# A hybrid-attention transformer layer on one core: paced first loads, key sets turned on VectorE

## The reference

```
u = rms_norm(h, g)
q, k_c, v_c, k_s, v_s, k_w, v_w, gate = split(u @ w_in)   # 16 query heads, 4 key/value groups of 128
k_c, v_c = compress(k_c), compress(v_c)                   # blocks of 32 tokens -> 15 compressed rows
k_s = rms_norm(k_s, g1);  k_w = rms_norm(k_w, g2)         # keys of the selected and the window branch
o = gate0*attn(q,k_c,v_c) + gate1*attn(q,k_s,v_s) + gate2*attn(q,k_w,v_w)
h = h + o @ w_out
h = h + square(relu(rms_norm(h) @ mlp_w1)) @ mlp_w2       # 2048 -> 8192 -> 2048
h = h + sigmoid(rms_norm(h) @ w_gate) * (p @ w_proj)
```

## Time and profile before

| | |
|---|---|
| median of 3 runs | 1208.8 us (1207.68 to 1210.01) |
| the profiled execution | 1206.92 us |
| its span, first to last instruction | 1204.8 us |
| TensorE busy | 1194.7 us (99%) |
| VectorE, ScalarE busy | 729.9 us (61%), 591.7 us (49%) |
| DMA in the first 30 us of the page's slices, then | 348 GB/s, then 283 and 210 |

### The profile page before, as it was taken

How to read it: one execution, slowest core, us unless ns; L and a number is a source line. 1 busy time by engine, 2 the same in 40 slices (tenths; PEclk the granted TensorE clock), 3 DMA queues, 4 the chain that set the end, 5 groups by cost and what they waited for, 6 DMA issues and landing times.

```text
span 1204.8 us, 15261 instructions
## 1 busy us (share of the span) xinstructions
PE 1194.7 (99%) x5504; PEld 992.3 (82%) x5504; DVE 729.9 (61%) x956; ACT 591.7 (49%) x812; POOL 70.6 (6%) x63
## 2 busy tenths in 40 slices
PE   8999999999999999999999999999999999999998
PEld 7888788888888888888888888888888888888886
DVE  5676646778766656554465554555555557476554
ACT  7655444666656554443444433445433444455443
POOL 1000000000000011100011100011000012000000
PEclk9999999999999999999999999999999999999999
DMA  9766564333348666765567765677755676785661
GB/s 348 283 210 217 176 202 135 118 106 106 112 152 267 221 222 217 248 226 195 193 211 260 237 207 192 190 242 236 241 192 196 207 242 221 248 263 194 217 206 49
DMA packets 107278, 247.02 MB, mean 205 GB/s; under 512 B 9424, under 2 KB 52432, under 8 KB 107216
## 3 DMA queue, kind: packets, MB, share of 16 engines
q1 hardware_dynamic: 107072, 246.24, 62.5%
q10 hardware_dynamic: 144, 0.01, 0.0%
HBM read 232.58 MB, written 13.63 MB: 204 GB/s over the span
## 4 chain that ended last, share of the span: by engine, by line
PE 94%; DVE 2%; ACT 1%; DMA 1%; SPq 1%; issue 0%; ACTq 0%
PE acc L1425 87%; PE sc L1566 1%; DMA x_raw<-in_x_cols_dram 1%; DVE w_split L947 1%; PE tr L1483 1%; ACT s L698 1%; PE sc L1531 0%; PE tr L1472 0%; PE sc L1472 0%; PE tr L1617 0%; PE tr L1618 0%; SPq L365 0%; PE acc L1455 0%; PE tr L1595 0%; ACT q_split L683 0%
## 5 line engine op out<-in xcount | busy, mean ns | idle before, releaser
L947 DVE TENSOR_TENSOR w_split<-w_raw,w_split 128x1024 fp32r<-128x1024 f32 x411 | 509.7, 1250 | 382.6 <-ACT w_split L597 382.1
L597 ACT ACTIVATE w_split<-w_raw 128x1024 fp32r<-128x1024 f32 x411 | 432.0, 1058 | 419.9 <-PE acc L1425 415.3
L1425 PE MATMUL acc<-w_split,a_hi 128*128 128x512 f32 x1916 | 594.5, 391 | 3.1 <-DVE w_split L947 3.1
L1425 PE MATMUL acc<-w_split,b_split 128*128 128x512 f32 x1920 | 441.0, 390 | 0.0
L1425 PEld LDWEIGHTS acc<-w_split,a_hi 128*128 128x128 f32 x1916 | 356.4, 188 | 78.3 <-issue 4.1
L1425 PEld LDWEIGHTS acc<-w_split,b_split 128*128 128x128 f32 x1920 | 359.4, 188 | 74.0
L1425 PE MATMUL acc<-w_split,a_lo 128*128 128x512 f32 x958 | 373.2, 390 | 0.0
L1425 PEld LDWEIGHTS acc<-w_split,a_lo 128*128 128x128 f32 x958 | 179.9, 188 | 37.7
L562 POOL TENSOR_TENSOR stage<-stage 128x512 f32<-128x512 f32 x32 | 49.8, 1574 | 559.1 <-ACT stage L605 559.1
L698 ACT ACTIVATE s<-s,nmx,q_scale 128x128 f32<-128x128 f32 (+1 forms) x64 | 34.2, 539 | 6.4 <-DVE nmx L1114 6.4
L605 ACT ACTIVATE stage<-acc,rstd 128x512 f32<-128x512 f32 x48 | 30.1, 678 | 10.1 <-PE acc L1425 9.6
(11 more groups left out here) (185 smaller groups left out, 515.9 us busy)
## 6 DMA issues: line engine op xcount, KB each, us to landing
w_raw<-in_mlp_w_units_dram SPq DMA_DIRECT2D x256, 512.0 KB, 4.3
w_raw<-in_nsa_w_in_units_dram SPq DMA_DIRECT2D x79, 512.0 KB, 4.3
w_raw<-in_nsa_w_out_units_dram SPq DMA_DIRECT2D x32, 512.0 KB, 3.7
w_raw<-in_ple_w_gate_units_dram SPq DMA_DIRECT2D x32, 512.0 KB, 4.2
turn_dram<-junk SPq DMA_DIRECT2D x44, 128.0 KB, 4.1
turn_dram<-s SPq DMA_DIRECT2D x44, 128.0 KB, 4.1
v_slc<-turn_dram SPq DMA_DIRECT2D x22, 256.0 KB, 4.0
v_win<-turn_dram SPq DMA_DIRECT2D x22, 256.0 KB, 4.4
```

What stands on the lines that cost most here:

```text
L597: nc.scalar.activation(w_hi[:, u % SPLIT], w_raw[:, u % RAW], ACT.Copy).then_inc(hi_done, 1)
L947: nc.vector.tensor_tensor(w_lo[:, u % SPLIT], w_raw[:, u % RAW], f32(w_hi[:, u % SPLIT]), ALU.subtract).then_inc(lo_done, 1)
L1425: last = nc.tensor.matmul(acc[c % 2][t][:], xs[:, kt, toks], ws[:, u % SPLIT, m * NW:(m + 1) * NW], start=(kt == 0 and n == 0), stop=(kt = ...
```

## The change

**First loads.** Unit KC1 is loaded in two halves with a semaphore each (`first_full`, `HALVED = 2`), and split in halves on ScalarE and VectorE, so that TensorE may start on its first half. The load of x for KC2 to KC7 now waits until the unit two before has landed (`raw_full[u - 2]`). `keep_busy` runs 8 matmuls in place of 10.

**Keys.** The sixteen transposes of the two key sets leave TensorE. VectorE turns the blocks (`keys_turn` behind KW4 and behind VS4), SyncE sends them to memory and fetches them back (`turn_away` behind the loads of VS0 and VW4, as `KEY_TURNS` says, `turn_back` two loads later), ScalarE and VectorE split them out of `p_t` (`keys_hi` in VS2 and VW5, `keys_out` in VS2 and VW6), VectorE with eight instructions a set in place of two. The compressed sets stay on TensorE.

**Parts of p.** `p_raw`, `pt_hi` and `pt_lo` lie over `p_t`, which is free after the attention; `p` is loaded behind the last load of `C_OUT+2`, after a wait on the last head (`o_done`), and split in `C_OUT+3`. The compressed keys' rows move to `junk_act` and `junk`.

```diff
@@ SyncE
-                        for m, full in enumerate((first_full, raw_full[0])):
+                        for m, full in enumerate((first_full[0], raw_full[0])):
...
                     if c == C_KC:
                         kts = slice(UNIT_KT * k, UNIT_KT * (k + 1))
+                        if k >= 2:
+                            sp.wait_ge(raw_full[u - 2], 16)
                         sp.dma_start(x_raw[:, kts], x_cols[:, kts]).then_inc(x_cols_full[k - 1], 16)
+                    if u < HALVED:
+                        for m, full in enumerate((first_full[u], raw_full[u])):
+                            sp.dma_start(slot(u)[:, m], packed(w_in_units, col // NW, k)[:, m]).then_inc(full, 16)
+                        continue
                     load(u, packed(w_in_units, col // NW, k), slot(u))
...
+                    for n, away in KEY_TURNS.items():
+                        if u == away:
+                            turn_away(n)
+                        if u == away + 2:
+                            turn_back(n)
...
-                        sp.dma_start(p_raw, p_cols).then_inc(p_full, 16)
+                    elif k == UPC - 1:
+                        sp.wait_ge(o_done, H)
+                        sp.dma_start(p_raw[:], p_cols).then_inc(p_full, 16)
@@ ScalarE
+            def keys_hi(n, br):
+                act.wait_ge(turn_in[n % 2], 16 * TT * (n // 2 + 1))
+                for t in range(TT):
+                    last = nc.scalar.activation(k_hi[:, :, t, br].rearrange("p m (g j) -> p m g j", j=QUAD),
+                                                turned_tiles(n)[:, :, 4 * t:4 * t + 4], ACT.Copy,
+                                                scale=const_t[:, GAIN_K + 1 + br:GAIN_K + 2 + br])
+                last.then_inc(turned_hi, 1)
@@ VectorE
+            def keys_turn(n):
+                dve.wait_ge(normed, n + 1)
+                turn_blocks(n, lambda t: stage[:, t])
+            def keys_out(n, br):
+                dve.wait_ge(turned_hi, n + 1)
+                for g in range(G):
+                    low = k_low(g // 2)[:, g % 2 * NW:(g % 2 + 1) * NW].rearrange("p (t b s) -> p t b s", t=TT, b=2)
+                    for t in range(TT):
+                        last = nc.vector.scalar_tensor_tensor(
+                            out=tokens(low[:, t, br]), in0=turned_tiles(n)[:, g, 4 * t:4 * t + 4],
                            scalar=const_t[:, GAIN_K + 1 + br:GAIN_K + 2 + br], in1=tokens(f32(k_hi[:, g, t, br])),
                            op0=ALU.mult, op1=ALU.subtract)
+                last.then_inc(turned_split, 1)
@@ TensorE
-            keep_busy(10)
+            keep_busy(8)
-                if k == 5:
-                    pe.wait_ge(normed, 1)
-                    transpose_set(R_KS, from_stage)
-                if k == 5:
-                    pe.wait_ge(normed, 2)
-                    transpose_set(R_KW, from_stage)
+                    if s == 8 and not g:
+                        pe.wait_ge(turned_split, T_KW + 1)
```

More of the change, by code:

```diff
@@ L93 @@
 _number_units()
+T_KS, T_KW, T_H1 = range(3)
+KEY_TURNS = {T_KS: FIRST[C_VS], T_KW: FIRST[C_VW] + 4}
 def pair_order():
@@ L106 @@
 LATE_UNITS = 4
-R_KC, R_VC, R_KS, R_KW = range(4)
+HALVED = 2
+R_KC, R_VC = range(2)
 def q_set(g):
-    return R_KW + 5 * g if g else R_KW + 1
+    return R_VC + 5 * g if g else R_VC + 1
 def p_set(h):
-    return R_KW + 1 + h + min((h + 1) // HPG + 1, G)
+    return R_VC + 1 + h + min((h + 1) // HPG + 1, G)
 R_H1 = p_set(H - 1) + 1
@@ L179, in trunk_layer @@
         s0 = sb("s0", [P, 2, 2, P])
+        with nc.sbuf_tensor("p_raw", [P, 2, SEQ], F32) as p_raw, \
+                nc.sbuf_tensor("pt_hi", [P, 2, SEQ], F32R) as pt_hi, nc.sbuf_tensor("pt_lo", [P, 2, SEQ], F32R) as pt_lo:
+            pass
         p_t = sb("p_t", [P, 2, NW + SEQ])
         p_cmp = sb("p_cmp", [P, 2, SEQ], F32R)
-        kc_rows, kc_sq = (p_t[0:N_CMP, b, 0:NW] for b in range(2))
+        kc_rows, kc_sq = junk_act[0:N_CMP], junk[0:N_CMP, 0:NW]
         mx = sb("mx", [P, 2, 4])
@@ L216, in trunk_layer @@
         tr = [pb("tr0"), pb("tr1")]
-        first_full = sem("first_full")
+        first_full = [sem(f"first_full{u}") for u in range(HALVED)]
         first_hi = sem("first_hi")
@@ L291, in trunk_layer @@
         turn_dram = nc.dram_tensor("turn_dram", (4, P // QUAD, QUAD, P // QUAD, TT, P), F32, kind="Internal").ap()
-        blocks = (junk[:], s1[:].rearrange("p a b s -> p (a b s)"))
-        turned = [v[:].rearrange("p t n -> p (t n)") for v in (v_slc, v_win)]
+        key_blocks = s1[:].rearrange("p a b s -> p (a b s)")
+        key_turned = p_t[:].rearrange("p b s -> p (b s)")[:, 0:TT * NW]
+        row_blocks = (junk[:], key_blocks)
+        row_turned = [v[:].rearrange("p t n -> p (t n)") for v in (v_slc, v_win)]
         block = ctx.enter_context(nc.Block())
@@ L323, in hid_sum, with blocks, turned @@
             return v_win[0:2 * HID + 1, kv, 0:DK]
+        def blocks(n):
+            return key_blocks if n < T_H1 else row_blocks[n % 2]
+        def turned(n):
+            return key_turned if n < T_H1 else row_turned[n % 2]
         def turned_tiles(n):
-            return turned[n % 2].rearrange("p (g m j) -> p m g j", m=NW // P, j=QUAD)
+            return turned(n).rearrange("p (g m j) -> p m g j", m=NW // P, j=QUAD)
         def tokens(x):
@@ L588, in split_hi @@
                     u = first + k
-                    if isinstance(i, int) and u == 0:
-                        act.wait_ge(raw_full[0], 16)
-                        nc.scalar.activation(w_hi[:, 0, NW:UW], w_raw[:, 0, NW:UW], ACT.Copy).then_inc(hi_done, 1)
+                    if isinstance(i, int) and u < HALVED:
+                        if u:
+                            first_half(u)
+                        act.wait_ge(raw_full[u], 16)
+                        nc.scalar.activation(w_hi[:, u, NW:UW], w_raw[:, u, NW:UW], ACT.Copy).then_inc(hi_done, 1)
                         yield k
@@ L1029, in staged_scale @@
                 heads_scale(n, stage_v, P, TT * HPG, normed)
-            def keys_out(r, br):
-                for b in range(2):
-                    dve.wait_ge(tr_hi[b], hi_sets(r))
-                    low = k_low(b).rearrange("p (g t b s) -> p g t b s", g=2, t=TT, b=2)
-                    nc.vector.scalar_tensor_tensor(
-                        out=low[:, :, :, br], in0=tr[b][:].rearrange("p (g t s) -> p g t s", g=2, t=TT),
-                        scalar=const_t[:, GAIN_K + 1 + br:GAIN_K + 2 + br], in1=f32(k_hi[:, 2 * b:2 * b + 2, :, br]),
-                        op0=ALU.mult, op1=ALU.subtract).then_inc(tr_done[b], 1)
+            def keys_turn(n):
[8 more added lines that the diff above has]
+                            out=tokens(low[:, t, br]), in0=turned_tiles(n)[:, g, 4 * t:4 * t + 4],
+                            scalar=const_t[:, GAIN_K + 1 + br:GAIN_K + 2 + br], in1=tokens(f32(k_hi[:, g, t, br])),
+                            op0=ALU.mult, op1=ALU.subtract)
+                last.then_inc(turned_split, 1)
             def queries_out(g):
@@ L1227, in _ @@
                     hidden_sum(1)
-                    keys_out(R_KS, 0)
+                    keys_out(T_KS, 0)
                 if k == 3:
@@ L1239, in _ @@
                     hidden_out(1)
-                if k == 7:
-                    keys_out(R_KW, 1)
             for k in split_lo(FIRST[C_VW], UPC):
@@ L1255, in _ @@
                 if k == 6:
-                    dve.wait_ge(p_hi, 1)
-                    nc.vector.tensor_tensor(pt_lo[:], p_raw, f32(pt_hi[:]), ALU.subtract).then_inc(p_split, 1)
+                    keys_out(T_KW, 1)
             for u in range(FIRST[C_GATE], END[C_GATE]):
@@ L1434, in half_unit @@
                     bank_free(c, i)
-                if m == 0 or kt == 1 and c == C_KC:
+                if c == C_KC and k < HALVED and m == 0:
+                    pe.wait_ge(first_lo, u + 1)
+                elif m == 0 or c == C_KC and k < HALVED:
                     pe.wait_ge(lo_done, u + 1 + 8 * UPC * i)
```

73 lines of the change are left out of this document (41 added, 32 removed).

## The result

| | before | after |
|---|---|---|
| median of 6 runs each, same chip | 1208.22 us (1206.97 to 1210.01) | 1214.06 us (1212.58 to 1216.68) |
| ratio, 95% interval | | 1.0051 [1.0042, 1.0061] |
| the profiled execution, its span | 1206.92, 1204.8 us | 1215.13, 1212.9 us |

The change makes the kernel 5.8 us slower. The prediction said 1208.5 us, in a range of 1206.2 to 1210.8. In the profiled executions TensorE's last matmul begins 8.07 us later than before. I lay TensorE's rows of the two traces side by side and ask at which places the distance between them grows.

The account below looks back on a forecast made before the run. TensorE, busy 1194.7 of 1204.8 us, was taken as the bound, with the transfers a limit beside it at the start. Terms +0.4 - 0.79 + 0.1 = -0.3 us gave a median of 1208.5 us, range 1206.2 to 1210.8.

Parts of the forecast that it names:

- From KC4 on each unit brings 1.31 MB, 3.3 us of moving, and the wait two units back costs nothing: First loads: from KC4 on, enough bytes move behind each landing to make the x loads' waits free.
- the one gap of 0.4 to 1.1 us: First loads: one pause in the full transfer stream, before the x load issued once KC1 has landed.
- the start +0.4: First loads: KC7 starts 0.4 us later than before, bounds -1.9 and +1.5.
- Rival (2): First loads: pacing starves the stream, a round trip per pair of units; pauses of 3.1 us give +2.4; chance 0.10.
- Rival (1): First loads: the start gain survives, KC7's data come sooner too; -2.6 us in all, 1206.2; chance 0.14.
- The eight in place of ten small matmuls ... Nothing: Start of TensorE: two fewer `keep_busy` matmuls only move its first four matmuls forward; no gain or loss.
- KC1 at 9.58 (predicted near 10.1): First loads: halving lets TensorE start KC1 near 10.1 us, 2 us sooner.
- TensorE's own limit: Start: TensorE's matmuls from KC1 on end at 28.7 us, KC7's data only 0.2 us later.
- The keys: Both key sets: first set -0.79 us with its transposes gone from TensorE; second set +0.1, VectorE having no room.
- waits in front of VS3 and VS4: Second key set: TensorE waits 0.8 to 1.2 us for VectorE's splits, which `keys_out` delays.
- The sum of the keys, -0.7: Both key sets together: -0.79 for the first and +0.1 for the second.
- Parts of p: Splits moved to `C_OUT+3`: no cost, units there have the split alone; without that cover, 0.7 us.

Follow-up runs that it names:

- a_unpaced: The changed kernel without the six waits of the x loads on the unit two before; 1210.22 us, ratio 1.0020.
- b_paced: The kernel before with only the six waits of the x loads added, KC1 in one piece; 1211.72 us, ratio 1.0026.
- a_pad10_vs: The changed kernel with five two-column padding matmuls on TensorE in front of VS3 and five in front of VS4; 1210.90 us, ratio 1.0018.
- a_pad10: The changed kernel with ten two-column padding matmuls (40 instructions) on TensorE between KC1 and KC2; 1209.25 us, ratio 1.0012.
- a_unpaced_pad10: The changed kernel without the x loads' waits and with ten padding matmuls between KC1 and KC2; 1208.17 us, ratio 1.0000.
- keys_only: The kernel before with only the keys and later p changed, no padding, 32 TensorE instructions fewer ahead of the loop; 1214.54 us, ratio 1.0060.
- keys_pad8: The kernel before with only the keys and later p changed, plus eight padding matmuls in front of KC1; 1207.89 us, ratio 1.000.
- b_nobusy: The kernel before without its ten small `keep_busy` matmuls, 40 TensorE instructions fewer; 1214.89 us, ratio 1.0053.
- b_h_late: The kernel before with the four pieces of h loaded behind KC7's weights; 1207.46 us, ratio 0.9996.
- h_late_pad10: The changed kernel without the x loads' waits, with ten padding matmuls between KC1 and KC2 and h loaded behind KC7's weights; 1208.15 us, ratio 0.9997.

## Why the prediction was wrong

**Where it failed: the pacing.** The step is the sentence "From KC4 on each unit brings 1.31 MB, 3.3 us of moving, and the wait two units back costs nothing", with the one gap of 0.4 to 1.1 us ahead of it; together they gave the start +0.4, at most +1.5. It measured +3.5 in the profile and +3.8 in two pairs of runs (after less a_unpaced, b_paced less before). I took the cost of an issue on a landing from a 192 KB load, 2.4 us. In the chain after, a unit's load of 0.5 MB took 5.6 to 7.3 us from issue to landing, and the half unit of 0.26 MB 5.0. And I held that enough bytes stood behind each landing, but the wait blocks everything behind it in the queue, h and the next units too, so the rate sank to 205 to 365 GB/s in all seven windows from 8 to 22 us. The gap was not where I put it, either: KC1 landed sooner than I had it, the next x was issued at 8.66, and the queue stood still one landing later, from 9.46 to 12.70. Rival (2) had this mechanism and nearly its size: four pauses of 0.9 us are 3.6, and 3.70 are missing in the windows. I gave it 0.10 because I compared one pause with 3.3 us of moving and did not lay out the chain of landings unit by unit.

The last x then is issued at 22.32, and its load still takes 5.21 us. Most of that is moving: some 1.5 MB, with a piece of h and KC6 in front of it, were not yet through, 3.8 us at the rates of the windows, and 1.4 us are the landing. Rival (1) drew on the Trainium skill, "DMA: Bandwidth & Descriptors", "Latency and other measured facts", for a fixed cost that is smaller under lighter load. The 1.4 us against 1.8 before point the way of that rule, but the transfers ran at 380 to 409 GB/s while this piece was under way, so no run here tests it.

**What was not in the sum: the loop.** No term, rival or bound spoke of TensorE's instructions themselves. I counted what the removed transposes and small matmuls took ("The eight in place of ten small matmuls ... Nothing") and not that 40 instructions fewer move the loop of the MLP against the 16 KB pieces in which they are fetched. In the profiled execution the two jumps back cost 1.8 and 1.7 us. By the medians it is 3.2 us (after less a_pad10_vs) to 4.8 (after less a_pad10), and in other kernels 2.1 (a_unpaced less a_unpaced_pad10) and 6.7 (keys_only less keys_pad8). The profiled executions tell the two kinds apart better than the medians: from 430 to 892 us TensorE falls back against the kernel before by 4.2 us in the changed kernel, 6.8 in a_unpaced, 8.0 in b_nobusy and 6.2 in keys_only, the four with 50 fetches, and by 0 to 2.4 in the eleven others with 32.

Together: -0.7 for the keys, +3.8 for the pacing, and the loop's 3.2 give +6.3, against 5.8 measured. The closeness owes something to the pairs chosen: with a_pad10's prices, 1.1 for the pacing and 4.8 for the loop, it is +5.2. That both causes are there is shown, how the loss divides between them only to about 2 us.

**What was right.** KC1 at 9.58 (predicted near 10.1), and its gain not kept: KC7 is bound by the last x, and TensorE's own limit lies 0.2 us beside it, which b_h_late shows. The keys: 0.79 us out of the stream for the first set; `keys_out` 2.1 us for its eight, mean 0.345 in the groups (predicted 0.35); waits in front of VS3 and VS4, and VS5 the moment its split ends. The waits are 0.75 and 0.37 us in place of 0.8 to 1.2, the second no longer than before. The sum of the keys, -0.7, was -0.8 in the profile and -0.69 in keys_pad8. So the Trainium skill's rule of "VectorE: DVE Perf Modes", "Rules for kernel authors", that gives a 128x128 transpose to TensorE, did not hold for the first set here, as the sum had it, by 0.8 us of 1208. Parts of p: no wait in `C_OUT+3`.

**What stays open.** Why the loop's place costs 2 us in one kernel and 7 in another, though part of it is TensorE's clock. The mean granted clock of every execution was recorded: of keys_only's five the one at 1.000 took 1211.86 us, three at 0.997 took 1214.4 to 1214.6, and the one at 0.995 took 1218.03; of the changed kernel's six the two at 1.000 were the fastest, 1212.58 and 1212.9, still over 5 us above the kernel before at the same clock (median 1207.3). Open too: why waits for VectorE of 0.4 to 1.0 us between 500 and 860 us turn up in the executions of some kernels and not of others; how many instructions between 8 and 32 move the loop over its border; and how much of the changed kernel's median is owed to the lower clock at 200 us, seen in its profiled execution and not in those of a_pad10 or keys_only.

## What to carry to other kernels

A wait on a landing in a queue that runs full holds back everything behind it, and the stream thins: here six such waits took 3.7 us of full-rate moving out of 14, and the chain of landings had links of 5.0 to 7.3 us. Before calling such a wait hidden, write down the issue and landing of each load unit by unit. When instructions are taken out of the engine that runs without idle time, compare the page's rows of instruction fetches, and look for waits "for issue" behind the jumps of its loops; a few instructions of padding in an idle place (in a stream without gaps each of these small ones cost 0.2 us) tell whether the change was slow or only badly placed. Time an edit with the loop at its old place, or its gain of 0.7 us drowns in 6.

## What the runs showed of the hardware

- TensorE went through a long loop again without any fetch, a pass of 176 us: 32 pieces of 16 KB in the whole run of the kernel before, none of them between 590 and 960 us. A shift of 32 to 40 instructions made it 50 pieces, with stalls of 0.9 to 3.65 us behind the jumps back. A stall "for issue" in the middle of an even stream of matmuls is the mark of it.
- The granted clock fell to 0.50, the level of 1.2 GHz, behind 2.6 us without a matmul in the changed kernel, and to 0.57 on average in a stretch of h_late_pad10, where TensorE had worked in all of the two us ahead. At that level a pair of matmuls took 1.19 us in place of 0.70. At the start it set no time, since TensorE waited for data anyway; near 200 us it cost 1.6 us. Behind the 2.74 us stall of a_unpaced it fell too (0.60 from 782 to 786).
- A padding matmul of two columns took 0.2 us of TensorE's stream, however little it multiplies. Ten of them are twenty matmuls and twenty weight loads of 128 x 128; the weight loads take 2.44 us in the trace, the stream 2.15.
